# Chunk inverses kept as packed 32x32 quarters, and within-block sums with the selection as weights

## The chip, the core and the metric

The kernel runs on one core of a Trainium2 chip, as one launch. The metric is device time in microseconds (us); less is better. The engines in this text are PE (TensorE, matmuls), DVE (VectorE), ACT (ScalarE), POOL (GpSimd) and SP (SyncE, which here only starts transfers). PE multiplies a stationary tile (the weights of an instruction) with a moving one and writes the product to one of eight banks of accumulation memory, of 128 partitions by 512 values.

## What is computed

The input has 256 tokens of 1024 channels. A first block of two layers, each a hybrid mixer (gated delta rule with 4 heads of 128, and dilated attention with 8 heads of 64) and a gated FFN with a short convolution, is followed by a second block of one layer: gated linear attention (GLA, 4 heads), a convolution of 31 taps, differential attention and a mixture of 16 experts. The change touches the inverse of `tri` in the delta rule, and the scores of GLA:

```python
    # gated delta rule, chunks of C = 64 tokens, for each head and chunk
    a_kk = jnp.where(strict, jnp.einsum('bhnid,bhnjd->bhnij', kb, k) * gamma, 0.0)
    tri = a_kk + jnp.eye(C, dtype=f32)
    sol = lax.linalg.triangular_solve(tri, rhs, left_side=True, lower=True, unit_diagonal=True)
    ...
    # gated linear attention, a decay for each channel d of the 32 of a head
    diff = b[:, :, :, None, :] - b[:, :, None, :, :]
    decay = jnp.exp(jnp.where(causal[:, :, None], diff, -jnp.inf))
    scores = jnp.einsum('bhik,bhjk,bhijk->bhij', qi, ki, decay)
```

## The kernel before

**Weights and precision.** Large matrices are multiplied as three products of rounded halves (high by high, high by low, low by high; `product`, lines 1776 to 1778). Weight tiles come from memory into a ring; ACT rounds a tile to its high half (`make_hi`, L2224), DVE makes the low half (`make_lo`, L2542), and PE uses them from three slots. `refill(n)` on ACT and on DVE is the place in each engine's queue where tile n is made. Each engine runs its own list in the order of the code, and semaphores tie them together.

**The mixer of a layer.** Behind the projections come, for each of 4 heads, `by_token` (transposes to token order) and `gram` (products of keys with keys and queries), lines 1928 and 1937. POOL and DVE make from them `bp`, which holds `a_kk` turned, for 8 units `u` (4 heads by 2 halves of 128 tokens), as matrices of 128x128 that hold two chunks of 64 on their diagonal. The inverse is built in blocks of doubling size: T is the inverse so far (`tinv`), U its transpose (`uinv`). Level 0 is two masks and a subtraction on DVE, which give U; a turn (`transposed(0, ...)`, L1864) gives T. The rounds `lev` 1 to 4 (`WIDE` is 5) then are, for two groups of four units:

- X: `bl` (the part of `bp` for this level, masked by POOL for lev 2 to 4) times T, line 2047, into banks 6 and 7, which ACT copies to `xs`;
- a score of the dilated attention (`scores`, L1869 and L1870), and from round 2 a turn of T into U, which ACT copies (L2418);
- Y: U times X, line 2057, into banks 0 and 1, which DVE subtracts from T (L2764);
- the values of an attention pair (`values(lev)`), with DVE's mask and norm of a pair beside them.

One more turn ends the rounds. The level from 32 to 64 works on quarters of 32x32 (lines 2072, 2083, 2085, 2090), the sum for 64 on halves (2102, 2111), and line 2118 starts the recurrence with `uinv` and `vb`. The last two weight tiles of the projections (the attention's values of heads 4 to 7, `late_values`) are multiplied behind the products of line 2072, 48 products in all, and ACT takes them from bank 5 into `vtok`.

**The second block.** Its projections and taps run in steps u = 0 to 27. In step 20 (`U_WITHIN`) PE multiplies the first tile of convolution taps, three products a tap (L707 to L709); steps 21 and 22 are token products, 23 to 27 the other taps. For GLA, `g_pr[:, r]` holds the products of keys, queries and decay for token distance r inside a block of 16, with 128 channels (4 heads of 32) on the partitions. Their sums over the channels of a head are 32 products (`within_rows`, L671) in each of steps 20 and 21, two behind each tap or token product: `g_pr` of 128 tokens is stationary, and `selhead` (4 columns, a head's selection) is moving. DVE reads the result in `within_blocks`. Norms and decays go from DVE or ACT back to PE through spreads (L1840), small products that write a row of factors to all partitions: `unit_inverse` (around 835 us of the span) and the end of step 27 (o_inv, L1485 and L1487, around 908 us) are such places; the decays of GLA (`log_decays`) stand in DVE's queue in step 6.

## Time and profile before

| | us |
|---|---|
| median of 3 runs (1144.71 to 1146.35) | 1144.74 |
| profiled execution, whole | 1145.11 |
| profiled execution, span of the trace | 1143.3 |
| PE busy in the span | 1114.1 (97%) |
| DVE, ACT, POOL busy | 805.3, 704.2, 60.1 |

Busy time is the union of an engine's instructions. The granted clock of PE was 0.999 of full speed over the whole span. Times in the rows below are from the start of the span; layer 0's mixer has its rounds from 114.60 to 142.06 us, and the second block's steps 20 and 21 are at 859 to 874 us. The file's lines in rows of the trace (L2047) are those of the listing above.

### The profile page before, as it was taken

The page shows a single profiled execution, that of the slowest core. Times are in us where ns is not written, and L with a number is a line of the kernel's source. Part 1 is how long each engine was busy: PE and PEld are TensorE (multiplying, and loading weights), DVE is VectorE, ACT ScalarE, POOL GpSimd, SP SyncE. Part 2 cuts the span into 40 slices and gives each one's busy share as a digit, 9 for nine tenths or more (in the row PEclk, how much of TensorE's full clock was granted, in tenths as well). Part 3 has the DMA queues.
Part 4 walks back from the last instruction along what each step waited for, and adds up shares of the span by engine and source line. Part 5 has one row for each costly group of instructions (what it writes and reads, how often), then busy time and mean ns, then how long its engine had stood idle before and what let it go on. Part 6 is the DMA issues. An engine that isn't in the chain of part 4 may idle for free. (4 is left out here: it accounts for less than half of the span.)

```text
span 1143.3 us, 21329 instructions
## 1 busy us (share of the span) xinstructions
PE 1114.1 (97%) x7888; PEld 1014.1 (89%) x7888; DVE 805.3 (70%) x1313; ACT 704.2 (62%) x1243; POOL 60.1 (5%) x97
## 2 busy tenths in 40 slices
PE   8999999999999999999999999999999999999998
PEld 8998888999999899978889999998989878888886
DVE  5866646877777896574587777776875658668995
ACT  6674665655555776465576555566954548457774
POOL 0002500000000000160030000000000000000000
PEclk9999999999999999999999999999999999999999
DMA  7653103556556455410346665663532306867991
GB/s 259 190 148 93 56 20 129 178 185 190 175 186 192 136 171 149 147 46 29 113 132 194 184 194 174 188 190 115 149 115 88 112 21 238 312 203 267 358 359 65
DMA packets 50664, 184.31 MB, mean 161 GB/s; under 512 B 5664, under 2 KB 5824, under 8 KB 50464
## 3 DMA queue, kind: packets, MB, share of 16 engines
q1 hardware_dynamic: 49680, 180.17, 48.8%
q0 software_dynamic: 912, 3.16, 0.8%
q8 instruction: 47, 0.77, 0.3%
q14 instruction: 25, 0.20, 0.1%
HBM read 182.27 MB, written 1.05 MB: 160 GB/s over the span
## 5 line engine op out<-in xcount | busy, mean ns | idle before, releaser
L2542 DVE TENSOR_TENSOR w<-ring,w 128x1024 fp32r<-128x1024 f32 x240 | 292.8, 1221 | 120.4 <-ACT w L2224 120.3
L1776 PE MATMUL bank<-act,w 128*128 128x256 f32 x1216 | 347.7, 286 | 5.2 <-DVE act L2566 4.3
L1778 PE MATMUL bank<-act,w 128*128 128x256 f32 x1216 | 343.7, 283 | 0.0
L1777 PE MATMUL bank<-act,w 128*128 128x256 f32 x1216 | 343.7, 283 | 0.0
L2224 ACT ACTIVATE w<-ring 128x1024 fp32r<-128x1024 f32 x240 | 252.5, 1053 | 83.4 <-PE bank L1778 64.8
L1776 PEld LDWEIGHTS bank<-act,w 128*128 128x128 f32 x1216 | 232.6, 191 | 8.9 <-issue 6.6
L1777 PEld LDWEIGHTS bank<-act,w 128*128 128x128 f32 x1216 | 232.7, 191 | 1.8
L1778 PEld LDWEIGHTS bank<-act,w 128*128 128x128 f32 x1216 | 232.8, 191 | 0.0
L2846 DVE SCALAR_TENSOR_TENSOR region<-bank,pf,region 128x255 f32<-128x255 f32 (+1 forms) x176 | 84.9, 482 | 36.2 <-ACT region L2499 25.5
L1776 PE MATMUL bank<-w,hid 128*128 128x512 f32 x206 | 81.6, 396 | 0.0
L1778 PE MATMUL bank<-w,hid 128*128 128x512 f32 x206 | 81.6, 396 | 0.0
L1777 PE MATMUL bank<-w,hid 128*128 128x512 f32 x206 | 81.3, 395 | 0.0
L2499 ACT ACTIVATE region<-bank,pf 128x256 f32<-128x256 f32 x88 | 49.4, 562 | 49.0 <-PE bank L1778 44.0
L1776 PE MATMUL bank<-w,act 128*128 128x256 f32 (+1 forms) x208 | 73.2, 352 | 0.0
L1778 PE MATMUL bank<-w,act 128*128 128x256 f32 (+1 forms) x208 | 69.1, 332 | 0.0
L1777 PE MATMUL bank<-w,act 128*128 128x256 f32 (+1 forms) x208 | 69.0, 332 | 0.0
L2509 ACT ACTIVATE hid<-region 128x256 fp32r<-128x256 f32 x42 | 17.6, 420 | 66.8 <-DVE region L2828 66.8
L1778 PEld LDWEIGHTS bank<-w,hid 128*128 128x128 f32 x206 | 38.8, 189 | 9.3
L1777 PEld LDWEIGHTS bank<-w,hid 128*128 128x128 f32 x206 | 38.9, 189 | 7.7
L1776 PEld LDWEIGHTS bank<-w,hid 128*128 128x128 f32 x206 | 38.9, 189 | 7.5
L1776 PEld LDWEIGHTS bank<-w,act 128*128 128x128 f32 x208 | 39.4, 189 | 6.2 <-issue 1.7
L1778 PEld LDWEIGHTS bank<-w,act 128*128 128x128 f32 x208 | 39.4, 189 | 4.0
(455 smaller groups left out, 2013.7 us busy)
## 6 DMA issues: line engine op xcount, KB each, us to landing
ring<-wtiles SPq DMA_DIRECT2D x240, 512.0 KB, 3.5
ring<-etiles SPq DMA_DIRECT2D x33, 512.0 KB, 4.9
act_raw<-etiles SPq DMA_DIRECT2D x33, 512.0 KB, 5.0
sq<-etiles SPq DMA_DIRECT2D x22, 512.0 KB, 5.2
cst<-etiles SPq DMA_DIRECT2D x8, 512.0 KB, 5.0
region<-packp POOLq DMA_DIRECT2D x4, 512.0 KB, 3.9
cst<-consts SPq DMA_DIRECT2D x1, 1348.0 KB, 11.2
x<-xt SPq DMA_DIRECT2D x2, 512.0 KB, 5.4
```

Source lines behind the costliest of these rows:

```text
L1776: t.matmul(out_, still[:, 0], moving[:, 0], start=first, stop=False)
L1777: t.matmul(out_, still[:, 0], moving[:, 1], start=False, stop=False)
L1778: return t.matmul(out_, still[:, 1], moving[:, 0], start=False, stop=last)
L2224: a.activation(w_hi[:, s, :], ring[:, s, :], ACT.Copy).then_inc(hi_ready, 1)
L2499: a.activation(dst[:, q, :], bank[UP_BANKS[2 * q + w]][:, 0:S], ACT.Identity, scale=pf_("conv", p * 6 + w * 3 + 2), bias=pf_("bias", p * 2 ...
L2509: a.activation(last_hi if late else hid_hi[:, q, :], glu_p[:, q, :], ACT.Copy).then_inc(hi_done, 1)
L2542: v.tensor_tensor(w_lo[:, s, :], ring[:, s, :], w_hi[:, s, :].bitcast(F32), ALU.subtract).then_inc(lo_ready, 1)
L2846: ins = v.scalar_tensor_tensor(dst[:, q, j:], src[:, 0:S - j], pf_("conv", p * 6 + w * 3 + 2 - j), dst[:, q, j:], ALU.mult, ALU.add)
```

## The change

T and U of all units now are kept as four quarters of 32x32, the diagonal of each 128x128, side by side (`tu`, with w = 0 for T and 1 for U; `xk` for X, `bpk` for `bp`, `bl` for the masked levels). `quarters` multiplies them as 16 products of 32x32 for a group of four units. Y now has two parts, U by X and X turned by U, so T and U are both updated by one subtraction and no turn is left but the first. Of the late values the half for tokens 0 to 127 now stands among the last `by_token` and `gram` and ahead of the rounds; the other half stays. ACT copies the four quarters of U into `uinv` behind the rounds, DVE two of T into `t64`, a new buffer. POOL masks the three levels one after another, ahead of its products for the heads. `weigh` of the attention stands one round later on ACT. The constants shrink, `level` from 7 x 128 to 5 x 32 columns, and `uinv` and `t64` are cleared by POOL at the start.

In the second block `selpad` (44 columns, the head's selection with zeros on both sides) is stationary in a window of 32 columns, and `g_pr` moves with 256 tokens: 16 products in four column quarters of bank 4, ACT's copy to `g_sq`, and two products with columns of `ident` that turn the sums into the old layout, all in step 20. Further, on DVE `unit_inverse`, `difference(3)` and a new `lengths_inverse` (remaining taps, o_inv, sum of the convolution) stand ahead of the refill of their step, and the refill of step 6 inside `log_decays`; on ACT the root for `d_rms` (step 14), `weigh(7)` (step 24) and the root and bias of step 27 stand ahead of the refill. The core of the diff:

```diff
+            def within_rows():
+                pe.wait_ge(pr_ready, GB // 4)
+                pe.wait_ge(st_copied, 3)
+                for k in range(4):
+                    still = cc("selpad")[:, SEL_AT - 4 * k:SEL_AT - 4 * k + 32]
+                    for q in range(4):
+                        mm = t.matmul(bank[4][32 * q:32 * q + 32, S:2 * S], still, g_pr[:, 4 * q + k, :],
+                                      start=k == 0, stop=k == 3)
+                mm.then_inc(st_done, 1)
...
+            def within_keys():
+                pe.wait_ge(st_copied, 4)
+                used = ident.rearrange("p (q n) -> p q n", q=4)[:, :, 0:4 * GH]
+                for jt in range(NT):
+                    mm = t.matmul(bank[4][:, jt * GB * GH:(jt + 1) * GB * GH], g_sq[:, 0, jt * P:(jt + 1) * P], used,
                                   start=True, stop=True)
...
-                        if u == U_WITHIN:
-                            within_rows(0, i)
+                        if u == U_WITHIN and i == 1:
+                            within_rows()
+                        if u == U_WITHIN and i == KD - 2:
+                            within_keys()
...
+                if u == U_WITHIN - 1:
+                    act.wait_ge(st_done, 4)
+                    a.activation(g_sq[:, 0, :], bank[4][:, S:2 * S], ACT.Copy).then_inc(st_copied, 1)
...
+            def lengths_inverse():
+                some_taps(len(DVE_TAPS))
+                dve.wait_ge(hn_std, 2)
+                ch.mark(v.reciprocal(o_inv, o_rms))
+                ch.dep()
+                v.tensor_scalar(o_inv, o_inv, 1.0 - LAMBDA_INIT, None, ALU.mult).then_inc(hn_inv, 1)
+                dve.wait_ge(cy_part, 1)
+                dve.wait_ge(tile_done, T2 + U_WOUT)
+                dve.wait_ge(cy_ready, 1)
+                v.tensor_tensor(c_y[:, 0, :], c_y[:, 0, :], bank[5][:, 0:S], ALU.add).then_inc(cy_ready, 1)
...
-                if u in AT:
-                    refill(AT[u])
                 if u == U_OG:
                     unit_inverse()
+                if u == 24:
+                    difference(3)
+                if u == U_STEPS - 1:
+                    lengths_inverse()
+                if u in AT and u != U_CONV + 4:
...
+                def late_values(c, half, part=range(KD // 2)):
+                    n, here = T_LATE + half, slice(c * P, (c + 1) * P)
+                    if c == 0 and 0 in part:
+                        tile_in(l * LAYER_TILES + n)
+                    for i in part:
+                        k, both = half * (KD // 2) + i, slice(i * S, (i + 1) * S)
+                        mm = product(bank[5][:, c * S:(c + 1) * S], act_both[:, :, k, here], w_both[:, :, n % SLOTS, both],
+                                     k == 0, k == KD - 1)
...
+                pe.wait_ge(bc_act, l * 4 + 3)
+                pe.wait_ge(bc_dve, l * 4 + 3)
                 for i in range(2, DNH):
+                    late_values(0, 0, range(2 * i - 4, 2 * i - 2))
                     by_token(i)
                     gram(i)
+                late_values(0, 1)
...
+                def quarters(out_, at, still, moving, g):
+                    for u in range(4 * g, 4 * g + 4):
+                        for q in range(4):
+                            mm = t.matmul(out_[quarter(q), packed(at + u % 4, B)], still(u, quarter(q)), moving(u, quarter(q)),
+                                          start=True, stop=True)
+                    return mm
                 pe.wait_ge(bc_act, l * 4 + 4)
                 pe.wait_ge(bc_dve, l * 4 + 4)
+                for g in range(2):
+                    pe.wait_ge(u_ready, first_u + g + 1)
+                    quarters(bank[g], 0, uk, lambda u, rows_: ident[rows_, rows_], g).then_inc(lev_t, 1)
...
+                        quarters(bank[6 + g], 0, lambda u, rows_: bl[rows_, lev - 1, u, :], tk, g).then_inc(lev_x, 1)
                     score(lev)
-                    if lev > 1:
-                        transposed(lev - 1, tinv, lambda g: (t_ready, first_t + 2 * (lev - 1) + g + 1))
                     for g in range(2):
-                        pe.wait_ge(u_ready, first_u + 2 * (lev - 1) + g + 1)
                         pe.wait_ge(lev_xs, first_x + 2 * (lev - 1) + g + 1)
-                        for u in range(4 * g, 4 * g + 4):
-                            mm = t.matmul(bank[g][:, u % 4 * P:u % 4 * P + P], uinv[:, u, :], xs[:, u, :],
-                                          start=True, stop=True)
-                        mm.then_inc(lev_y, 1)
+                        quarters(bank[g], 0, uk, lambda u, rows_: xk[rows_, u, :], g)
+                        quarters(bank[g], 4, lambda u, rows_: xk[rows_, u, :], uk, g).then_inc(lev_y, 1)
+                    if lev == 4:
+                        pe.wait_ge(proj_evac, l * 16 + 15)
                     values(lev)
...
+                        a.activation(xk[:, 4 * g:4 * g + 4, :], half(bank[6 + g]), ACT.Copy).then_inc(lev_xs, 1)
+                    weigh(lev - 1)
...
+                for q in range(4):
+                    ins = a.activation(uinv[quarter(q), :, quarter(q)].rearrange("p (g u) k -> p g u k", g=2),
+                                       tu[quarter(q), :, 1], ACT.Copy)
+                ins.then_inc(u_ready, 1)
...
+                        for q in range(4):
+                            ch.mark(v.tensor_copy(bpk[quarter(q), us, :], bp[quarter(q), us, quarter(q)]))
+                        ch.dep()
+                        ch.mark(v.tensor_tensor(tu[:, g, 1], bpk[:, us, :], level(0), ALU.mult))
+                        v.tensor_tensor(bl[:, 0, us, :], bpk[:, us, :], level(1), ALU.mult).then_inc(bl_ready, 1)
+                        ch.dep()
+                        v.tensor_tensor(tu[:, g, 1], cc("eye").unsqueeze(1).to_broadcast([P, 4, B]), tu[:, g, 1],
+                                        ALU.subtract).then_inc(u_ready, 1)
...
+                        v.tensor_tensor(tu[:, g], tu[:, g], bank[g][:, 0:S].rearrange("p (w u k) -> p w u k", w=2, k=B),
                                         ALU.subtract).then_inc(t_ready, 1)
+                    masked(lev)
...
+                pool.wait_ge(bl_ready, l * WIDE + 2)
                 for lev in range(2, WIDE):
-                    if lev == 2:
-                        pool.wait_ge(u_ready, l * 2 * LEVELS + 2)
-                    else:
-                        pool.wait_ge(lev_x, l * 2 * (LEVELS - 1) + 2 * (lev - 2))
-                    pl.tensor_tensor(bl[:, lev % 2], bp[:],
-                                     cc("level", lev, P).unsqueeze(1).to_broadcast([P, NT * DNH, P]),
+                    pl.tensor_tensor(bl[:, lev - 1], bpk, cc("level", lev, B).unsqueeze(1).to_broadcast([P, NT * DNH, B]),
                                      ALU.mult).then_inc(bl_ready, 1)
```

On PE, layer 0's mixer, from the first turn to the second Y. Before (`cst` is the identity, `sq` holds T, `y` the masked levels, `h` the attention's queries and keys, `region` the rest):

```order
L1864 MATMUL bank<-cst,region 128x128 x8
L2047 MATMUL bank<-sq,y 128x128 x8
L1869 MATMUL bank<-h 128x128
L1870 MATMUL bank<-h 128x256
L2057 MATMUL bank<-sq,region 128x128 x8
L2047 MATMUL bank<-sq,y 128x128 x8
L1869 MATMUL bank<-h 128x128
L1870 MATMUL bank<-h 128x256
L1864 MATMUL bank<-cst,sq 128x128 x8
L2057 MATMUL bank<-sq,region 128x128 x8
```

After, with a score behind the first turn instead of ahead of it:

```order
L2084 MATMUL bank<-cst,sq 32x32 x32
L1915 MATMUL bank<-h 128x128
L1916 MATMUL bank<-h 128x256
L2084 MATMUL bank<-sq,y 32x32 x32
L1915 MATMUL bank<-h 128x128
L1916 MATMUL bank<-h 128x256
L2084 MATMUL bank<-sq 32x32 x64
L2084 MATMUL bank<-sq,y 32x32 x32
L1915 MATMUL bank<-h 128x128
L1916 MATMUL bank<-h 128x256
L2084 MATMUL bank<-sq 32x32 x64
```

The turn ahead of the second Y is gone, X has 32 products of 32x32 for 8 of 128x128, and Y 64 for 8.

On PE in the second block, step 20, before (`hid` and `thin` hold the parted convolution input, L754 is the differential attention of the step ahead):

```order
L754 MATMUL bank<-region 128x64 x7
L707 MATMUL bank<-hid,w 128x256
L708 MATMUL bank<-thin,w 128x256
L709 MATMUL bank<-hid,w 128x256
L671 MATMUL bank<-cst,region 128x4 x2
L707 MATMUL bank<-hid,w 128x256
```

After:

```order
L789 MATMUL bank<-region 128x64 x7
L739 MATMUL bank<-hid,w 128x256
L740 MATMUL bank<-thin,w 128x256
L741 MATMUL bank<-hid,w 128x256
L739 MATMUL bank<-hid,w 128x256
L740 MATMUL bank<-thin,w 128x256
L741 MATMUL bank<-hid,w 128x256
L695 MATMUL bank<-region,cst 32x256 x16
L739 MATMUL bank<-hid,w 128x256
```

The sums come once, behind the second tap, where before two small products stood behind every tap of this step and every product pair of the next.

On DVE in step 27, before (L2542 is `make_lo` of a weight tile, L1305 the taps of DVE, L1483 the convolution's sum, L1485 and L1487 o_inv):

```order
L2551 TENSOR_TENSOR act<-mix,act 128x256 x2
L1305 SCALAR_TENSOR_TENSOR region<-region,pb 128x256 x2
L2542 TENSOR_TENSOR w<-ring,w 128x1024
L1305 SCALAR_TENSOR_TENSOR region<-region,pb 128x256 x2
L1483 TENSOR_TENSOR region<-region,bank 128x256
L1485 RECIPROCAL region<-region 128x8
L1487 TENSOR_SCALAR region<-region 128x8
L2542 TENSOR_TENSOR w<-ring,w 128x1024
```

After:

```order
L2592 TENSOR_TENSOR act<-mix,act 128x256 x2
L1345 SCALAR_TENSOR_TENSOR region<-region,pb 128x256 x4
L1469 RECIPROCAL region<-region 128x8
L1471 TENSOR_SCALAR region<-region 128x8
L1475 TENSOR_TENSOR region<-region,bank 128x256
L2583 TENSOR_TENSOR w<-ring,w 128x1024 x2
```

The two weight tiles moved behind the inverse and the sum, and the inverse ahead of the sum.

## Rows read from the trace of the kernel before

**Rows 1.** the page's first part: busy time, share of the span, instructions
```profile
PE 1114.1 (97%) x7888; PEld 1014.1 (89%) x7888; DVE 805.3 (70%) x1313; ACT 704.2 (62%) x1243; POOL 60.1 (5%) x97
```

**Rows 2.** by stretch: length, each engine's busy us (instructions), clock, DMA
```profile
104.45:114.60 10.15, 9.23 (x60) 7.80 (x59) 7.82 (x22) 7.67 (x27) 2.98 (x4) 1.00 0.05 18
114.60:142.06 27.46, 26.09 (x206) 22.67 (x205) 18.09 (x40) 16.52 (x43) 15.04 (x21) 1.00 0.17 58
142.06:150.06 8.00, 8.00 (x86) 7.36 (x85) 1.79 (x6) 2.62 (x8) 0.00 (x0) 1.00 0.01 2
```

**Rows 3.** PE's waits in layer 0's mixer: for whom, us, times, longest
```profile
PE bank L2057 <- ACT region L2418: 0.8, 3, 0.3
PE bank L1864 <- DVE region L2731: 0.6, 1, 0.6
PE bank L1864 <- ACT region L2373: 0.5, 1, 0.5
PE bank L1869 <- ACT region L2376: 0.4, 1, 0.4
```

**Rows 4.** PE in time order, round 1 and small products: start, us
```profile
116.36 2.01 PE L2047 MATMUL bank<-sq,y 128*128 128x128 f32 x16
118.30 0.48 PE L1869 MATMUL bank<-h 64*128 64x128 f32 x2
119.14 2.05 PE L2057 MATMUL bank<-sq,region 128*128 128x128 f32 x16
121.20 2.02 PE L2047 MATMUL bank<-sq,y 128*128 128x128 f32 x16
...
142.06 1.09 PE L2072 MATMUL bank<-sq,region 32*32 32x32 f32 x32
```

**Rows 5.** PE's groups, 114.60 to 142.06: the last four turns
```profile
L1864 PE MATMUL bank<-cst,sq 128*128 128x128 f32 x32 | 4.4, 279 | 0.0
```

**Rows 6.** PE in time order, three streams of 32x32 products at once
```profile
149.73 0.28 PE L1777 MATMUL bank<-w,act 128*128 128x256 f32 x1
149.85 0.28 PE L1778 MATMUL bank<-w,act 128*128 128x256 f32 x1
...
150.46 0.19 PE L2083 MATMUL bank<-sq,region 32*32 32x32 f32 x1
150.47 0.19 PE L2085 MATMUL bank<-region,sq 32*32 32x32 f32 x1
150.47 0.21 PE L2090 MATMUL bank<-region,sq 32*32 32x32 f32 x1
150.49 0.19 PE L2083 MATMUL bank<-sq,region 32*32 32x32 f32 x1
```

**Rows 7.** ACT in time order: one copy of 128x128 out of a bank
```profile
105.62 0.28 ACT L2361 ACTIVATE region<-bank 128x128 f32<-128x128 f32 x1 [2.22 <-PE bank L1966]
```

**Rows 8.** DVE in time order: a round's subtractions, and a product beside POOL
```profile
120.37 0.68 DVE L2764 TENSOR_TENSOR sq<-sq,bank 128x512 f32<-128x512 f32 x1
122.03 2.00 DVE L2752 TENSOR_SCALAR region<-region 128x128 f32<-128x128 f32 x1
```

**Rows 9.** PE in time order in the second block, step 20
```profile
861.02 0.36 PE L707 MATMUL bank<-hid,w 128*128 128x256 f32 x1
861.45 0.50 PE L671 MATMUL bank<-cst,region 128*128 128x4 f32 x4
861.81 0.36 PE L707 MATMUL bank<-hid,w 128*128 128x256 f32 x1
```

**Rows 10.** by stretch, line 864 alone (router, four column quarters): PE, PEld
```profile
935.50:935.60 0.10, 0.10 (x12) 0.10 (x8) 1.00 0.00 0
```

**Rows 11.** PE in time order in the second block: three waits, in brackets
```profile
811.12 0.36 PE L1776 MATMUL bank<-act,w 128*128 128x256 f32 x1 [0.85 <-DVE w L2542]
...
835.29 3.71 PE L1840 MATMUL bank<-cst,region 128*64 128x128 f32 x64 [1.14 <-DVE region L1389]
...
908.36 2.05 PE L1840 MATMUL bank<-cst,region 128*128 128x128 f32 x16 [1.24 <-DVE region L1487]
```

More of the change, by code:

```diff
@@ L2089, in layer @@
                 for u in range(2 * DNH):
-                    mm = t.matmul(bank[7][quarter(2), packed(u, 32)], xs[quarter(3), u, 0:32],
-                                  uinv[quarter(3), u, quarter(3)], start=True, stop=True)
+                    mm = t.matmul(bank[7][quarter(2), packed(u, B)], xs[quarter(3), u, 0:B],
+                                  uk(u, quarter(3)), start=True, stop=True)
                 mm.then_inc(lev_y, 1)
@@ L2412, in small, with half @@
                     return b[part, 0:2 * DNH * 32].rearrange("p (u k) -> p u k", k=n)
[L2414 to L2418 removed]
+                def half(b):
+                    return b[:, 0:4 * B].rearrange("p (u k) -> p u k", k=B)
                 first_x, first_y = l * 2 * (LEVELS - 1), l * 2 * (LEVELS - 1)
[L2421 to L2422 removed]
+                for g in range(2):
+                    act.wait_ge(lev_t, l * 2 + g + 1)
+                    a.activation(tu[:, g, 0], half(bank[g]), ACT.Copy).then_inc(t_ready, 1)
+                act.wait_ge(late_done, l + 1)
+                a.activation(vtok[:, 0, S:2 * S], bank[5][:, 0:S], ACT.Copy).then_inc(proj_evac, 1)
                 for lev in range(1, WIDE):
@@ L2885, in _ @@
             pool.dma_start(pa[:], packa[0]).then_inc(packa_in, 16)
+            pl.memset(uinv, 0.0)
+            pl.memset(t64[:], 0.0)
             pl.memset(rows[:], 0.0).then_inc(zeroed, 1)
```

238 lines of the change are left out of this document (99 added, 139 removed).

## Prediction

> **What bounds the kernel.** The page's first part comes first: PE is busy for 1114.1 of 1143.3 us [rows 1]. So work taken off PE is worth its time, unless a wait takes its place, and other engines matter where PE waits. The busy time by stretch then gives the two places of the change in each layer: the stretch of rounds (114.60 to 142.06, PE busy 26.09 of 27.46) and the 8.00 us behind it, all busy; in both DVE and ACT are busy for two thirds of the time or less, and the clock is at 1.00, the upper level of 2.4 GHz [rows 2]. PE's waits in the mixer sum to 2.3 us [rows 3]. They are the same four in the second layer, so every figure for a layer counts twice.
>
> **One layer: what goes.** A round is X (B times T, line 2047), a score, Y (line 2057), and from round 2 a turn of T. Start to start X takes 118.30 - 116.36 = 1.94 and Y 121.20 - 119.14 = 2.06 [rows 4]: four rounds, 16.0. The last four turns are 4.4 us busy [rows 5], 1.1 each, of which about 0.1 lies under what follows; with the first, 5 x 1.0 = 5.0. Together 21.0. Line 2072 walks 32 records down one place of the array in 1.09 us [rows 4]; its two places now alternate: 0.5 less. The waits of 2.3 go: three are for copies of turns that no longer exist, the others come ahead of the rounds, where the late values now stand. These are 48 products at 0.12 [rows 6], 5.8 us, the same before and after; half of them, 2.9 us, now fill the time in which DVE masks. Gone: 21.0 + 0.5 + 2.3 = 23.8.
>
> **What comes.** The unit is 16 products of 32x32 for four blocks and four quarters, 32 records. There are 2 for the first turn, 2 in each X, 4 in each Y: 2 + 8 + 16 = 26 units, 832 records a layer. No row shows four such places at work. One place alone gives a record every 0.032 us (1.03 / 32, line 2072 from its start to the next line), which would be 1.03 a unit. Two places give two per 0.03 us, 0.52. Around 150.47 three run together, three records per 0.03 us, and none slows [rows 6]: 0.32. Four would give 8 x 0.032 = 0.26. I take 0.30, nearest to the three streams: 26 x 0.30 = 7.8.
> The array's shape changes more often, twice more in rounds 2 to 4 and twice outside, 8 x 0.1 = 0.8 (a triple of 0.36 takes 0.43 ahead of another shape [rows 9]; 0.1 is the same, rounded up). Behind a wait the first small weight load is not hidden, 0.1 in some 8 places: 0.8.
> New waits. A round is a chain: the last record and its tail (0.19 long, 0.03 to the next [rows 6], so 0.16), DVE's subtraction (0.42, my estimate for half the size of today's 0.68 [rows 8]), two semaphores, about 0.7 in all to X of the second group. X of the first group (0.3) and the values' transposes (0.4) lie beside it in rounds 2 to 4; between rounds 1 and 2 nothing does: 0.3. X's copy to Y is 0.28 [rows 7] beside a score of 0.84: hidden. The masks: for the last pair of heads DVE needs a product, four small copies, two masks and a subtraction, by my estimate 1.9 us behind the last Gram product; late values of 1.4 and the first unit cover it but for 0.45. The first late value behind the rounds waits for the evacuation of the first attention pair (0.25), one X copy behind a weight conversion 0.2. Together 1.2.
> DVE was 18.1 us busy in the stretch of rounds and ACT 16.5 [rows 2]. DVE loses 2.4 (eight subtractions of half the size), 1.7 (a slow product, below) and 2 (masks now done ahead): 12. ACT loses ten turn copies (0.54 each, my estimate: four times the size of [rows 7] for twice its 0.28) and a cut of eight X copies to a quarter (0.3 each): 8.7. PE takes about 14.5 for the four rounds, so neither binds, DVE being the nearer. ACT's four copies into uinv fall beside the late values; the two copies and the negation into t64 stand behind mask 5 and norm 4 on DVE and are ready about 1.5 us before PE asks. On POOL three masks of a quarter the size replace three of 2 us; the heads' products behind them end earlier.
> Layer: 23.8 - 7.8 - 0.8 - 0.8 - 1.2 = 13.2 us, twice 26.4.
>
> **The second block.** A step of a tap triple with two of the old sums takes 861.81 - 861.02 = 0.79, the triple alone 0.36 [rows 9], so 16 steps give back 16 x 0.43 = 6.9, and the 0.3 us wait ahead of them is passed under the first triples. In comes 16 products with 32 columns of weights and 256 moving ones, 32 records. The router's product is of this shape with 128 columns: 12 records of 0.27 us touch a stretch of 0.1 [rows 10], one per 0.37 / 12 = 0.031; twice the columns, 0.062 each, 2.0 us. Changes of shape 0.2, the two turning products 0.3; ACT's copy between them (0.4) lies under five tap triples. Net 4.7. If only two column places work at once the 32 records cost 3.4 (0.107 each), and the net is 3.3.
> The three waits of 0.85, 1.14 and 1.24 [rows 11] stand behind DVE or ACT work that now comes earlier: the weight part ahead of the reciprocal's users, the root ahead of the refill and of the last decays, the length inverse ahead of refill and convolution sum. What is queued behind the moved steps are refills, late by 0.7 to 1.6 us for weights due three tiles (9 us) on. Of 3.2 I count 3.0. Steps 20 to 24 get shorter by 5 us in sum, and DVE's refill, mask and difference (about 4 us a step) still end before the tile that needs them. Second block: 7.7.
> The constants shrink by 340 KB, loaded behind the first weights: nothing, at most 0.5.
>
> **Sum.** The profiled execution took 1145.1 us (1143.3 in its span, 1.8 around it), 0.4 above the median of 1144.7. 1145.1 - 26.4 - 7.7 = **1111**, the 0.4 left inside the rounding.
>
> **Rivals.**
> *Records come out at two streams' pace.* If what three streams show is a short burst from a full queue and the queue feeds one record per 16 ns, a unit is 0.52, 26 x 0.22 = 5.7 more a layer, of which 0.6 takes the place of waits: 1111 + 10.2 = 1121. For it: the burst is 0.1 us long [rows 6]. Against: nothing slows in it. Chance 0.22.
> *Other engines bind.* A DVE product of 128x128 took 2.00 us beside a POOL product of that length, where a subtraction of four times its size takes 0.68 [rows 8]. The new POOL products are 0.7 long, but small copies and norms meet more of them; 0.5 a round, and refills late in the second block, add 8: 1119. Chance 0.06.
> *A floor of the issue, or the clock.* At 25 ns a record, a unit is 0.80, the layer gains 1.2 instead of 13.2: 1135; half the clock in the rounds would double 13 us of PE's work and give a similar 1137. For it nothing in the rows: records are 10 ns apart where three places run, and the clock stays at 1.00 through stretches of small products [rows 2]. Chance 0.04.
> *The quarters exclude each other.* All four write one bank, each its own partitions; the streams of [rows 6] write different banks. If one waits for the other, a unit is 1.03, 26 x 0.73 = 19 more a layer, 1 of it in place of waits: 1111 + 36 = 1147; with a weight load of 0.1 exposed at each of four changes of place a unit, 10 a layer, 1168. It decides where a unit costs (33.8 / 2 + 1) / 26 = 0.69 more than my 0.30, at 1.0. Chance 0.06: 0.02 of it within 0.2%, 0.04 above.
> The Trainium skill (TensorEngine Tiling (Array Packing), Restrictions and Gotchas) has the rule behind this: different row tiles cannot access the same PSUM bank at the same time. No run here shows it for quarters that also differ in columns; by that rule the sum would be this rival's. The skill's TensorE: Matmul & The Clock Gate (Wait — 56ns, not 53.3ns?) puts the least distance of matmuls at about 25 ns; by it the sum would be the third rival's 1135, and the trace has them closer where places differ, 10 ns, so I follow the rows.
>
> **How the numbers follow.** Forecast 0.62, two streams 0.22, engines 0.06, floor or clock 0.04, exclusion 0.06. Four at full pace (26 x 0.04 = 1.0 a layer more), every wait gone and 0.5 at the start give 1108; 1 to 2 us less of new waits 1106. The two streams' case with half-parallel columns (1.4) and half the waits (1.5) ends at 1124; with the engines' delay added in part, 1127. 1106 to 1127 leaves out 0.10 and some edges. A difference within 0.2% (2.3 us) can't be told from none here. Faster 0.62 + 0.22 + 0.06 + 0.04 = 0.94, same 0.02, slower 0.04.
>
> **What would show it.** Units of 0.3 us: the 64 records of an X within 0.7 us and the 128 of a Y within 1.3, rounds of 3.3 to 3.8 instead of 6.3. From the first Gram product to the product of uinv and vb PE takes 13 us less, with waits of about 1.2. In the second block the column products take about 2 us, and no wait of 1 us stands at the spreads. I would be wrong if record distances in a unit exceed 15 ns, if DVE or ACT follow each other without a gap in the rounds, or if the weights come late in steps 21 to 27.

## The result: 1136.2 us, and the profile after

The changed kernel took 1136.22 us (median of 5 runs, 1131.96 to 1140.26); the kernel before took 1145.18 beside it. The ratio is 0.9888, with a 95% interval of 0.9846 to 0.9931. The forecast was 1111, with a range of 1106 to 1127. The change is faster, by a quarter of what was forecast. Its runs spread over 8 us where those of before spread over 1.6, and that spread is a part of the finding. Beside later kernels some executions show a lower mean clock than the others and take longer (for the kernel before 1154 to 1160 us at 0.986 to 0.990, against 1144 to 1148 at 0.997 or more), so the ratios below that rest on many of them have wide intervals, and three such runs of the one-place order (1167 to 1170 us) are left out of its figures.

The first part of the page shows PE busy for as large a share of its span as in [rows 1], with 1300 more records:

```profile
span 1130.2 us, 23915 instructions
...
PE 1096.9 (97%) x9188; PEld 997.1 (88%) x9188; DVE 794.6 (70%) x1321; ACT 694.4 (61%) x1236; POOL 53.1 (5%) x99
...
PEclk9999689999999999997999999999999999999999
```

The clock row has a 6 and a 7, in the rounds of the two layers, where the kernel before has only nines. The stretches of [rows 2] after the change (PE, PEld, DVE, ACT, POOL busy, each with its count, then the granted clock, DMA share and GB/s):

```profile
104.45:114.60 10.15, 10.15 (x74) 9.29 (x73) 5.88 (x21) 7.67 (x27) 2.93 (x4) 1.00 0.04 16
114.60:142.06 27.46, 21.82 (x874) 17.07 (x874) 13.41 (x40) 9.09 (x31) 10.89 (x21) 0.67 0.20 61
142.06:150.06 8.00, 8.00 (x84) 6.91 (x82) 2.78 (x11) 4.55 (x15) 0.00 (x0) 0.65 0.01 2
```

The late values fill the stretch ahead of the rounds, as forecast. In the rounds PE now is idle for 5.6 of 27.5 us, and its mean clock is 0.67. The same queue in order of time, from the second round on (start, us, then shape and count, and in brackets the idle time before it and its releaser):

```profile
121.25 0.45 PE L2084 MATMUL bank<-sq,y 32*32 32x32 f32 x32 [0.20 <-DVE sq L2807]
121.64 0.48 PE L1915 MATMUL bank<-h 64*128 64x128 f32 x2
121.96 0.59 PE L1916 MATMUL bank<-h 64*128 64x256 f32 x2
122.48 0.31 PE L2084 MATMUL bank<-sq 32*32 32x32 f32 x11
123.94 1.82 PE L2084 MATMUL bank<-sq 32*32 32x32 f32 x117 [1.15 <-issue]
125.69 0.90 PE L1910 MATMUL bank<-cst,region 128*128 128x128 f32 x3
126.52 0.33 PE L2084 MATMUL bank<-sq,y 32*32 32x32 f32 x8
127.60 0.97 PE L2084 MATMUL bank<-sq,y 32*32 32x32 f32 x56 [0.75 <-issue]
128.50 0.79 PE L1915 MATMUL bank<-h 64*128 64x128 f32 x2
129.09 1.06 PE L1916 MATMUL bank<-h 64*128 64x256 f32 x2
130.08 1.17 PE L2084 MATMUL bank<-sq 32*32 32x32 f32 x68
133.53 1.07 PE L2084 MATMUL bank<-sq 32*32 32x32 f32 x60 [2.29 <-issue]
```

Two things are to be seen. PE stands in the middle of a Y, and no engine releases it: "issue" is time in which nothing that the profile shows was awaited. And from stand to stand there are 117 + 3 + 8 = 128 records, then 56 + 2 + 2 + 68 = 128; to the stand of 0.75 us ahead of the score at 137.19 it is 127, and a trace can miss a record. The four stands of the first layer sum to 4.9 us, the five of the second (0.28, 0.63, 2.17, 1.53, 0.80) to 5.4. The score's two products took 0.84 us before and take 128.50 to 130.08, 1.58, here: the clock is at its lower level. Where it is, by windows laid on its edges:

```profile
119.00:123.80 4.80, 3.53 (x209) 2.66 (x208) 3.00 (x8) 2.52 (x10) 4.58 (x10) 1.00 0.01 3
123.80:147.70 23.90, 19.97 (x577) 16.29 (x577) 8.76 (x25) 8.84 (x27) 3.55 (x7) 0.50 0.22 70
505.00:509.50 4.50, 2.33 (x191) 1.99 (x192) 2.54 (x8) 0.42 (x2) 3.68 (x8) 1.00 0.14 15
509.50:523.10 13.60, 11.27 (x366) 8.65 (x354) 5.39 (x14) 4.14 (x15) 0.00 (x0) 0.50 0.35 117
925.90:929.30 3.40, 3.40 (x18) 3.40 (x18) 2.59 (x14) 0.00 (x0) 0.00 (x0) 0.51 0.21 19
```

A mean of 0.50 is 1.2 GHz: 23.9 us in the first layer, 13.6 in the second, and 3.4 at the router, where the kernel before kept 2.4 GHz. (The short one needs no packed rounds: the kernel below with the old rounds and the new order has one of 3.4 us at 947.6.)

By landmarks, the product of `uinv` and `vb` starts at 156.48 us for 156.69 before, a gain of 0.2 in the first layer where 13.2 was forecast. The same product of the second layer starts 3.9 us earlier, and the span ends 13.1 earlier, so 9.2 came behind it. Of the 3.9, 1.0 was not the mixers' own: PE's dense work between the two layers' mixers ran that much faster, in the kernel with the old rounds too, as the account below shows. The two mixers gave 2.9.

### The profile page after: what moved, and what is told of

Read it like the earlier page. It is cut to its first block, busy times and chain, and to the rows that moved or that the text cites. A ratio compares the mean times of both kernels' runs of the same rounds, so it can differ in the third digit from the quotient of the medians.

```text
span 1130.2 us, 23915 instructions
## 1 busy us (share of the span) xinstructions
PE 1096.9 (97%) x9188; PEld 997.1 (88%) x9188; DVE 794.6 (70%) x1321; ACT 694.4 (61%) x1236; POOL 53.1 (5%) x99
## 4 chain that ended last, share of the span: by engine, by line
PE 93%; ACT 2%; DVE 2%; issue 2%; DMA 1%; SPq 0%; DVEq 0%
PE bank L1822 25%; PE bank L1823 25%; PE bank L1824 25%; PE bank L2084 2%; PE bank L1910 2%; PE bank L1886 2%; PE bank L1877 1%; PE bank L1916 1%; PE bank L1915 1%; ACT sq L2278 1%; PE bank L1002 1%; DMA x<-xt 1%; PE bank L1970 1%; PE bank L739 1%; PE bank L921 1%
## 5 line engine op out<-in xcount | busy, mean ns | idle before, releaser
L1822 PE MATMUL bank<-w,hid 128*128 128x512 f32 x206 | 80.8, 392 | 0.0
L1823 PE MATMUL bank<-w,hid 128*128 128x512 f32 x206 | 80.6, 391 | 0.0
L1824 PE MATMUL bank<-w,hid 128*128 128x512 f32 x206 | 80.2, 389 | 0.0
```

The costliest lines, as they stand in the source:

```text
L1822: t.matmul(out_, still[:, 0], moving[:, 0], start=first, stop=False)
L1823: t.matmul(out_, still[:, 0], moving[:, 1], start=False, stop=False)
L1824: return t.matmul(out_, still[:, 1], moving[:, 0], start=False, stop=last)
```

## The experiments

Medians are of 4 to 10 runs, and each ratio is to the kernel before on the same chip; medians of different kernels were in part taken on different chips. "Stands" are PE's idle time put down to issue, in both layers' rounds.

### The second block alone

```diff
-                        if u == U_WITHIN:
-                            within_rows(0, i)
+                        if u == U_WITHIN and i == 1:
+                            within_rows()
+                        if u == U_WITHIN and i == KD - 2:
+                            within_keys()
...
+                if u == U_STEPS - 1:
+                    lengths_inverse()
+                if u in AT and u != U_CONV + 4:
```

> The second block's part of the change alone, on the kernel before (sums by column quarters, and the moved steps of DVE and ACT; the rounds stay as they were). By the trace of after, PE reaches the router 10.1 us earlier than the rounds' own gain explains, and loses 0.9 us again to a clock of 1.2 GHz just behind it. If that stretch of half clock was chance, this kernel takes 1145.2 - 10.1 = 1135; if it belongs to the second block's change, 1136. The clock is 0.999 or 1.00 in both layers' rounds. Of the change's 9 us nothing would then come from the rounds.

It took **1133.83** (1133.67 to 1134.64), ratio 0.989 (0.9874 to 0.9907): as fast as the whole change (1136.2 and, timed again below, 1132.3), with a clock of 1.00. In its profile PE's waits of [rows 11] are gone. What the sums cost is best seen in the changed kernel, where they are the same (step 20, PE in time order):

```profile
852.97 0.29 PE L739 MATMUL bank<-hid,w 128*128 128x256 f32 x1
...
853.45 1.93 PE L695 MATMUL bank<-region,cst 128*32 128x256 f32 x32
855.32 0.39 PE L739 MATMUL bank<-hid,w 128*128 128x256 f32 x1
```

The 16 products take 1.87 us (forecast 2.0). Steps 20 and 21 together, from the first tap to step 22's first product, went from 16.2 us to 11.3: 4.9, forecast 4.7.

### The rounds alone

```diff
-                        if u == U_WITHIN and i == 1:
-                            within_rows()
-                        if u == U_WITHIN and i == KD - 2:
-                            within_keys()
+                        if u == U_WITHIN:
+                            within_rows(0, i)
...
-                if u in AT and u != U_CONV + 4:
+                if u in AT:
```

> The rounds' part of the change alone: packed quarters, late values and POOL's order, with the second block as before. The changed kernel gained 9 us and the second block alone 12, so this part alone should lose about 2 to 3: 1146 + 2.5 = 1148.5, between 1143 and 1153, with stretches of 1.2 GHz in both layers that differ from run to run. If the two parts lean on each other (the second block's gain needing the earlier arrival), it would be 1140 or less, or over 1155.

It took 1143.69 (1141.55 to 1154.82), ratio 0.9968 (0.9922 to 1.0013): no difference that can be told. Its clock was at 1.2 GHz for 13.7 us in the first layer and 23.9 in the second, and its stands sum to 9.8 us. My expectation of a loss of 2 to 3 rested on two medians from different chips; the two parts add up within their spread. Its profile has 3.4 us at 1.2 GHz in the second block too, at 872.0, though that block is the old one here.

### The post norms' loads behind the rounds

```diff
                 pool.wait_ge(kbg_ready, l * 4 + 4)
+                pool.wait_ge(lev_y, l * 2 * (LEVELS - 1) + 2 * (WIDE - 1) + 1)
                 for i, row in enumerate((post_mix, post_ffn)):
```

> The changed kernel with POOL's two loads of the post norms (1 MB, 3.5 us of DMA) issued behind the rounds instead of inside them. Theory of supply: PE stands in the rounds since its next 16 KB of instructions has not come, and the longest stand of each layer (2.29 and 1.53 us) is one whose fetch waited behind this burst; then these two shrink to the size of the others (0.7 to 1.2), the sum of PE's stands without a releaser falls from 10.3 to about 8.5 us, and the time falls by 1.5 to 2.5. If the stands have another cause, they stay, and so does the time. The clock falls to 1.2 GHz in the rounds as before by either theory.

It took 1129.79 (1128.34 to 1139.38), ratio 0.9879 (0.9833 to 0.9925). The stand of 2.29 us in the first layer and that of 1.53 in the second are gone; in the first layer the one behind grew from 0.75 to 0.89 and a new one of 1.33 came, and the sum fell from 10.3 to 7.5 (8.5 had been expected). The changed kernel's own DMA shows why. In three windows of the DMA queues, 121.7 to 121.8, 127.6 to 131.2 and 131.2 to 131.3 us (queue, packets, MB, share of 16 engines):

```profile
q8 instruction: 1, 0.02, 59.9%
...
q0 software_dynamic: 281, 1.04, 86.2%
...
q8 instruction: 1, 0.02, 59.3%
```

PE's instructions come in packets of 16 KB on q8: the change has 1300 more products' records, as many weight loads, and ten more such packets in the span (57 for 47), 260 instructions for each. Before the first layer's four stands they start at 117.8, 121.8 and 125.1; the next starts at 131.2, when nearly all of the burst of q0 is through, and then come 134.6 and 138.2. Each takes 0.9 to 1.3 us. All nine stands of the two layers end 1.2 to 1.5 us behind the end of a packet. And a packet starts only when PE has gone on from a stand: 1.0 to 1.1 us behind the stand's end in seven cases, but 3.65 and 2.8 in the two in which the burst was on the queues. So from going on to being able to go on again takes 3.3 us or more, and 128 small records last 1.4.

The timing alone is unsure, since one of the four runs took 1139.4. Of the two stands, only the first is surely the burst's: a second profile of the unedited change (its run stands at the end of this section) has the same 2.29 in the first layer, but 0.23 where the 1.53 was, since its packet started 2.1 us behind and not 2.8:

```profile
512.18 1.18 PE L2084 MATMUL bank<-sq 32*32 32x32 f32 x70 [0.23 <-issue]
```

Its stands sum to 8.5 us with nothing changed, so a difference of a microsecond or two between two sums is no finding.

### No second half of Y

```diff
-                        quarters(bank[g], 0, uk, lambda u, rows_: xk[rows_, u, :], g)
-                        quarters(bank[g], 4, lambda u, rows_: xk[rows_, u, :], uk, g).then_inc(lev_y, 1)
+                        quarters(bank[g], 0, uk, lambda u, rows_: xk[rows_, u, :], g).then_inc(lev_y, 1)
...
+                        v.tensor_tensor(tu[:, g, 0], tu[:, g, 0], bank[g][:, 0:P].rearrange("p (u k) -> p u k", k=B),
```

> The changed kernel without the second half of each Y (X turned by U, 64 of a round's 192 small records) and with DVE subtracting from T alone; U stays at level 0, so the later factors are other numbers. It leaves out 64 x 4 x 2 records, 5.8 us at full speed. Theory of supply: a third fewer instructions in a round, so stands of PE without a releaser fall from 10.3 us to under 3. The clock separates two theories: if it falls because PE stands idle in these gaps, it stays at 1.00 and the time is near 1111 - 6 = 1105; if it falls because small products count little, it still falls and the time is 1118 to 1126.

It took 1119.79 (1117.42 to 1122.13), in the range of the theory that small products lower the clock. It leaves out half of Y, so it is no alternative to the change. The stands fell from 10.3 to 6.5 only, less than expected: a third fewer instructions run in a shorter round. The clock fell in both layers, for 6.8 and 17.1 us, and in the second at 496.6 us, when PE had stood once, for 0.96 us, just before.

### Late values spread over the rounds

```diff
                     score(lev)
...
+                    for half, part in {1: ((0, range(0, 3)),), 2: ((0, range(3, 4)), (1, range(0, 2))), 3: ((1, range(2, 4)),)}.get(lev, ()):
+                        late_values(1, half, part)
...
-                late_values(1, 0)
                 score(WIDE)
-                late_values(1, 1)
...
+                pool.wait_ge(lev_y, l * 2 * (LEVELS - 1) + 2 * (WIDE - 1) + 1)
```

> The changed kernel with the 24 late value products of tokens 128 to 255 (2.8 us of PE, 48 instructions) set into rounds 1 to 3 instead of behind the rounds, and the post norms' loads behind the rounds. Same work, same number of instructions. Theory of supply: the large products give the fetch time, so the stands shrink from 10.3 us to 3 to 6, and by the theory that idle time lowers the clock it falls later or not at all: 1115 to 1125. If small products lower the clock by themselves, three large ones of 0.12 us in a round change it little, and the time is within 3 us of the changed kernel with later loads.

It took **1138.06** (1136.72 to 1138.84). This kernel has the later loads too, so its neighbour is the run above, on the same chip: 1129.79, with stands of 7.5 us. Spreading the late values made it 8 us slower and the stands 10.0, and neither theory had expected that. The clock fell later in the first layer, at 135.0, but then came back late: PE was at 1.2 GHz again from 145.2 to 158.9, and in the second layer from 520.7 to 544.6. Perhaps the dense late values behind the rounds are what brings the clock up soon; that is not tested by itself. So this edit moved the loss behind the rounds and made it larger.

### One place of the array at a time

```diff
-                    for u in range(4 * g, 4 * g + 4):
-                        for q in range(4):
+                    for q in range(4):
+                        for u in range(4 * g, 4 * g + 4):
```

> The changed kernel with the 16 products of a group ordered quarter by quarter, four after one another in one place of the array. Same products, same count. One place gave a record every 0.032 us in the kernel before, so a unit of 32 records takes 1.03 us instead of 0.34, and 123 records, the content of 16 KB of instructions, take 3.9 us, more than the 3.3 to 4.0 us between two fetches. Theory of supply: the stands without a releaser are gone (under 1 us in sum). A layer then has 26 x 0.69 = 18 us more of products for 5 us less of stands: about 1136 + 26 = 1162 if the clock behaves as before. Theory that idle time in the stands lowers the clock: it stays at 1.00 in both layers, and the time is 1145 to 1155. Theory that small products lower it: it falls in both layers though PE never stands, and the time is 1160 or more.

It took 1150.47 (1149.12 to 1159.57, seven runs), ratio 1.0044 (1.0003 to 1.0085). Its profile (a run of 1149.17) separates the two theories of the clock:

```profile
117.00:121.30 4.30, 4.30 (x137) 3.60 (x139) 1.17 (x3) 1.95 (x8) 4.18 (x9) 1.00 0.01 4
121.30:155.40 34.10, 34.10 (x728) 30.15 (x724) 11.58 (x33) 10.05 (x33) 5.50 (x11) 0.50 0.15 49
506.00:510.40 4.40, 4.40 (x136) 3.65 (x133) 1.17 (x3) 1.98 (x8) 4.32 (x9) 1.00 0.02 4
510.40:544.50 34.10, 34.10 (x745) 30.15 (x738) 11.59 (x33) 9.55 (x32) 5.78 (x12) 0.50 0.15 49
```

PE is busy for all of 34.1 us in each layer, and the clock is at 1.2 GHz for all of it. There is no stand: a record comes every 0.020 to 0.027 us at full clock, which lasts for the first 4.3 us only, and every 0.030 to 0.035 at the lower level, where the 128 of a Y take 4.2 us, and the fetch keeps up. So idle time is not needed for the clock to fall; a queue that is mostly 32x32 products is enough. And the stands are a matter of pace: they are gone with the same instructions at less than half the speed. The time that I had put beside the theory that holds, 1160 or more, was too high by 10 us; the time lies where I had put the other theory. I had priced a record at full clock at 0.032, and this order takes about 0.023.

### Twice the moving columns

```diff
...
-                            mm = t.matmul(out_[quarter(q), packed(at + u % 4, B)], still(u, quarter(q)), moving(u, quarter(q)),
+                            mm = t.matmul(out_[quarter(q), packed(at + u % 4, B * wide)], still(u, quarter(q)),
+                                          moving(u, quarter(q)).unsqueeze(1).to_broadcast([B, wide, B]),
                                           start=True, stop=True)
```

> The changed kernel with 64 moving columns in each 32x32 product of the rounds, the same 32 twice; the second copy lands in unused columns of the banks. Same instructions, twice the moving columns. In the records so far an X of 64 records takes 0.68 us at full clock. If only the instruction's own pace counts (0.011 us each), nothing changes in the rounds' products; if columns count too, an X takes up to 1.1 us. Theory of supply: the stands of PE without a releaser shrink by what the products take longer. Theory that idle time in those stands lowers the clock: it falls where it did, near the first long stand. Theory that the small products lower it, having few columns at work: it falls later or not at all, and the time is 1120 to 1130 though the products are longer.

With `wide` = 2, and work that nobody uses, it took **1127.51** (1126.57 to 1130.20), ratio 0.9817 (0.9762 to 0.9872), against 1132.3 and 1136.2 for two timings of the change. PE in time order, first round:

```profile
117.70 1.10 PE L2084 MATMUL bank<-sq,y 32*32 32x64 f32 x64
118.72 0.48 PE L1915 MATMUL bank<-h 64*128 64x128 f32 x2
119.05 0.59 PE L1916 MATMUL bank<-h 64*128 64x256 f32 x2
119.57 1.99 PE L2084 MATMUL bank<-sq 32*32 32x64 f32 x128
121.38 1.37 PE L2084 MATMUL bank<-sq,y 32*32 32x64 f32 x64
```

An X takes 1.02 us for 0.68, a Y 1.81 for 1.42. The clock fell at 135.6 and at 514.5, for 6.8 us each, instead of 23.9 and 13.6; two of the stands still are long (2.97 and 1.95 us).

### Useless large products between X and Y

```diff
                     score(lev)
...
+                    if lev < 4:
+                        for _ in range(6):
+                            t.matmul(bank[5][:, S:S + P], ident, ones, start=True, stop=True)
```

> The changed kernel with six more products of 128x128x128 (identity times ones, 12 records, 1.4 us) between X and Y in rounds 1 to 3, 8.6 us of useless work over both layers. Theory that small products lower the clock by themselves or by their short idle stretches: with every third microsecond full, the clock stays at 1.00 in most of the rounds, which gives back 8 to 12 us; the time is then 1130 to 1137. If the clock falls nevertheless, the filler costs 1.4 us (2.8 at half clock) each time, and the time is 1142 to 1150. Stands without a releaser shrink in both cases, since 24 instructions now take 1.4 us.

It took 1135.01 (1131.71 to 1136.03), ratio 0.988 (0.9822 to 0.9937): 8.6 us of useless work cost nothing that can be told. Time at 1.2 GHz was 20.5 us in the two mixers, for 37.5 in the change; the stands kept 3.0 and 6.3 us.

### Both cures at once

```diff
+                pool.wait_ge(lev_y, l * 2 * (LEVELS - 1) + 2 * (WIDE - 1) + 1)
...
+                                          moving(u, quarter(q)).unsqueeze(1).to_broadcast([B, wide, B]),
```

> The 64 column kernel of s6_wide with the post norms' loads behind the rounds as in s3_packp, both edits at once. Theory of supply: the stands of 2.97 and 1.95 us, each with its fetch behind that burst, shrink to about 1, which gives 2 to 3 us. Theory that the clock follows how much of the array's time is filled by columns: with the longest stand gone the clock falls in at most one of the layers, for a short stretch or not at all, which gives another 0 to 3. So 1127.5 - 2 to 6: 1121.5 to 1125.5. If the burst had nothing to do with the stands, 1127 or more.

It took **1124.90** (1123.84 to 1127.36), ratio 0.9774 (0.9717 to 0.9831): the fastest of all, 9 us better than the second block alone.

```profile
117.00:139.70 22.70, 19.27 (x838) 15.68 (x837) 12.68 (x36) 8.54 (x30) 8.53 (x17) 1.00 0.10 29
139.70:143.20 3.50, 3.48 (x15) 3.26 (x16) 0.06 (x1) 3.27 (x10) 0.00 (x0) 0.51 0.00 0
500.00:522.00 22.00, 17.67 (x601) 14.29 (x600) 10.65 (x30) 9.54 (x31) 3.05 (x7) 1.00 0.09 28
```

The clock holds through the rounds of both layers, and the longest stand is 1.49 us. The stands still sum to 6.3 us.

### Wide products in rounds 3 and 4 alone

```diff
...
-                        quarters(bank[g], 0, uk, lambda u, rows_: xk[rows_, u, :], g)
+                        quarters(bank[g], 0, uk, lambda u, rows_: xk[rows_, u, :], g, 1 + (lev > 2))
```

> As s10_wide_packp, but rounds 1 and 2 have 32 moving columns and only rounds 3 and 4 have 64. Rounds 1 and 2 are then 1.7 us shorter for each layer at full clock. If the clock is set by the last few microseconds alone and the wide rounds come in time, it falls no more than in s10_wide_packp and the time is 1 to 3 us lower. If columns in the first rounds matter, it falls in the first layer near 122 us, as in the changed kernel, and the time is 1 to 6 us above s10_wide_packp.

It took 1126.75 (1125.74 to 1128.19), ratio 0.9789 (0.9732 to 0.9846), 1.9 above the run before. The clock fell at 128.7 and 500.8 and stayed down for 3.4 and 10.2 us, not near 122 as I had written for the case in which the first rounds matter. The shorter first rounds were paid for by the clock; the stands (6.0 us) are as before.

### The change's order without its packing

```diff
                 for i in range(2, DNH):
+                    late_values(0, 0, range(2 * i - 4, 2 * i - 2))
                     by_token(i)
                     gram(i)
+                late_values(0, 1)
```

> The kernel of s1_second (rounds as before, second block changed) with the late values of tokens 0 to 127 moved ahead of the rounds as in the change. This is the change's order without its packing. The waits of 0.4 and 0.6 us ahead of the rounds in each layer are covered, and perhaps the 0.5 at the score; the three waits of 0.25 at Y stay, and one for the evacuation of bank 5 may come. So 1133.8 - 2 x 1.2 = 1131.4, between 1130.5 and 1133.5, with the clock at 1.00 in all rounds. If the moved products bring nothing, or put DVE's masks later, 1133.8 or more.

It took 1131.76 (1131.05 to 1132.43), ratio 0.9855 (0.98 to 0.9909), 2.1 us below the second block alone, as expected. The waits ahead of the rounds are gone, one of 0.3 us at the first X came, and those of 0.25 at Y stayed. This kernel, with the new second block and the new order but the old products, is as fast as the whole change. It is the fair base for the packing: as first written the packing gained nothing on it, and with the two edits above (1124.90) it gained 6.9 us.

### The changed kernel again

> The changed kernel once more, unedited, on the chip that runs the others of this call, to see how its time spreads: 1130 to 1141, with a mean clock of 0.975 to 0.983, where the kernels whose clock holds spread over 2 to 3 us. The stretches at 1.2 GHz should begin in other places than in its first profile, between the second and the fourth round of each layer, and the time should follow the mean clock: about 0.5 us for each microsecond at 1.2 GHz.

It took 1132.33 (1129.54 to 1135.24), ratio 0.9839 (0.978 to 0.9897). The clock fell at 123.0 and 505.3 (for 23.9 and 17.1 us), where the first profile has 123.8 and 509.5. Over the eleven runs of both timings the mean clock went from 0.984 at 1129.5 us to 0.975 at 1140.3; a line through them gives 0.43 us for each microsecond at 1.2 GHz (my estimate; 0.5 was expected), with up to 5 us left between runs of one mean clock. So the change is 9 us faster by the first timing and about 14 by this one, and most of the spread of its runs is how long the clock is down.

## Why the prediction was wrong

**What bounds the kernel:** held. PE is busy for 97%, and work taken off it would have been worth its time.

**The unit of 0.30 us:** nearly right. At full clock an X of two units took 0.68 and a Y of four 1.42, so 0.34 to 0.355 a unit. Four places run side by side, a record every 0.011 us, writing one bank. The rival in which quarters of one bank exclude each other is refuted: at full clock a record came every 0.020 to 0.027 us in the one-place order and every 0.011 in the four-place order. That is also the pace of the three streams of [rows 6]: the fourth place brought nothing more. The Trainium skill (TensorEngine Tiling (Array Packing), Restrictions and Gotchas) has different row tiles excluded from one bank at the same time; these quarters differ in rows and columns, and the trace shows no such wait. The price of the unit cost 26 x 0.05 x 2 = 2.6 us.

**The new waits (1.2 a layer):** too high. 0.44 and 0.20 us showed in a layer, 1.1 less over both.

**The step that failed** is the sum 26 x 0.30 taken as time. It priced a record by a burst and left out what a long row of such records does. Two things came on top, and neither had a term of its own:

- The supply of instructions. PE finds 256 instructions, 128 records of products and as many weight loads, in one 16 KB packet, and in the rounds a packet came every 3.3 to 4.0 us at the best. Four places use one up in about 1.4 us, one place, at the lower clock, in about 4.2. The first round and a half run from what had been fetched ahead; then PE stands at each packet's edge. It cost 4.9 and 5.4 us, of which the post norms' burst on the DMA engines, which falls into the same microseconds, made some 2.8 by the run without it, give or take the 1.8 by which two profiles of the same kernel differ. The kernel before uses a packet in 10 to 17 us and never shows this. The Trainium skill (Runtime: NRT & Kernel Launch, Instruction fetch mechanics) has the block of 16 KiB and 256 instructions, fetched while the one before it runs, and calls the cost of crossing it mostly hidden. The 128 records from stand to stand agree with the block; with four places at work the cost is not hidden.
- The clock. It was at 1.2 GHz for 37.5 us in the two mixers, and a queue of small products is enough for that, as the one-place order shows; whether the stands add to it in the four-place order is not separated. The forecast for the mixers was 26.4 and 2.9 were measured; with 10.3 of stands, 2.6 of dearer units and 1.1 of waits that did not come, about 26.4 - 2.9 - 10.3 - 2.6 + 1.1 = 11.7 us are left for it. The traces have the same sum by another way. Each record of the two stretches was laid beside the same record, or others of its line, at full clock, in this profile and in two others of this program order (the change again, and the later loads): they took 7.5 and 4.5 us longer, 12.0 in all, by this estimate. A 32x32 record went from 0.011 to 0.015 us, a 128x128 one from 0.12 to 0.24. Where the clock held (the run with both cures), this loss was gone though the products had grown by 0.73 us a round.

The third rival, a floor of the issue or the clock, ended at 1135 to 1137 and stood at 0.04. It was the nearest. Its half on the clock came true in part: it doubles 13 us of PE's work in each layer, 26 in all, and some 12 came. Its half on the floor did not come true as written: no record waits 25 ns for the one before, the supply does over 128 of them (3.5 us / 128 = 27 ns). That half the clock's loss and the supply's together ended near its figure for either alone is luck. My two reasons against it were that records stood 10 ns apart in [rows 6] and that the clock stayed at 1.00 in [rows 2]. The first is a burst, the second a stretch in which most of the time is 128x128 products. Neither row says anything on 20 us of 32x32 products, so they were no evidence, and the rival should have had a chance like that of two streams. The range, drawn by the bounds of one record's pace, had no room for it. And none of the three signs by which I would have seen myself wrong came: at full clock the records stood 11 ns apart, DVE and ACT did not bind, the weights came in time. All three looked at paces and engines, none at the supply or the clock.

**The second block:** right in kind, too low in sum. The steps of the sums gave 4.9 (forecast 4.7), the waits 3.8 (3.0). The block's part alone took 11.3 us less than the profiled execution of before, where 7.7 was forecast. The rest is 2.9, since 0.3 of the waits lies inside those steps, and most of it does not come in the second block's changed steps. With the same records laid side by side it is 0.9 between 210 and 385 us and 1.0 between 600 and 770, where PE is busy without a wait, and tenths elsewhere. In the first of these stretches some products of 512 moving columns follow at 0.227 us where the kernel before has 0.235. The same 0.9 and 1.0 are in all eight profiles with the new second block that were laid beside it (the change among them), and not in the one with the old block. What in the edit does it is open. In the changed kernel's profile about 1.2 us of the block's gain went again, in the 3.4 us of lower clock at the router.

**DVE and ACT** did not bind: 13.4 and 9.1 us busy in the rounds (forecast 12 and 8.7 for a shorter stretch).

A ledger for the fastest kernel, in which the clock holds, shows that nothing large is missing. Its products of `uinv` and `vb` come 10.2 us earlier in the second layer, 1.0 of which the second block's edits give too: 9.2 of 26.4. Wider products cost 8 x 0.73 = 5.8, stands 6.3, dearer units 2.6, a new wait for DVE 0.9, one stretch of 3.4 us at lower clock about 1, less the 1.1 of waits: together 24.7 of 26.4.

## What to carry to other kernels

Before many small products replace a few large ones, count PE's instructions against the packets in which they come, and look how long a queue of the new products would be, since a burst of ten records shows neither the fetch nor the clock. Where the array runs small tiles in parallel, more columns of the same instructions can be free or better than free. And time the parts of a change one by one: here one part carried nearly all of the measured gain, and the packing was worth something only after two more edits. Time its new order without it, too.

## What the runs showed of the hardware that I had not expected

- PE can starve for instructions with nothing else wrong: stands of 0.2 to 2.97 us, 128 records (or a multiple) apart. In the changed kernel each ended 1.2 to 1.5 us after the end of a 16 KB packet, and the next packet started 1.0 to 1.1 us after PE had gone on; a burst of 1 MB on the same DMA engines held one packet back by 2.5 us and another by 1.7.
- The granted clock fell to 1.2 GHz while the trace shows PE busy for 34.1 of 34.1 us. The Trainium skill (TensorE: Matmul & The Clock Gate, Part 1: The HAM clock gate) lets the chip set it by how busy PE has been; busy in the trace's sense is not that. What exactly it counts is left open here.
- Doubling the columns of every product in the rounds, for nothing, made the kernel 5 to 9 us faster.
- Quarters that differ in rows and columns write one bank side by side, a record every 0.011 us.
- At 1.2 GHz the four-place records came 1.4 times as far apart (0.015 us), the 128x128 ones twice (0.24): half the clock is not twice the time for small products.
